# A decoder layer on Trainium2: finishing of the four widest top-k selections spread over the sparse-attention steps, the fourth settled by itself

## The reference

```python
rel = jax.nn.relu(jnp.einsum('bthd,bsd->bths', iqb, ik).astype(jnp.float32))
score = jnp.einsum('bths,bth->bts', rel, iwb.astype(jnp.float32)) * idx_scale
score = jnp.where(causal[None], score, -jnp.inf)
_, sel = lax.top_k(score, n_sel)
...
logits = jnp.where(valid[:, :, None, :], logits, -jnp.inf)
p = jax.nn.softmax(logits, axis=-1).astype(v.dtype)
```

## Time and profile before

| what | value |
|---|---|
| median of 3 runs | 1570.82 us (1570.29 to 1573.15) |
| the profiled execution | 1571.99 us |
| its span, first to last instruction | 1570.2 us |
| mean granted TensorE clock | 0.975 |
| TensorE, VectorE, ScalarE, GpSimd busy | 94%, 70%, 32%, 48% of the span |

### The profile page before, as it was taken

The page is one execution under the profiler, slowest core; times in us unless marked ns, Lnnn a source line. Parts: engine busy times, 40 slices in busy tenths (PEclk is TensorE's granted clock), DMA queues, the critical chain, the costliest instruction groups (busy, mean ns, idle before and its releaser), DMA issues.

```text
span 1570.2 us, 21084 instructions
## 1 busy us (share of the span) xinstructions
PE 1476.6 (94%) x7552; PEld 1255.9 (80%) x7552; DVE 1097.7 (70%) x2104; ACT 498.5 (32%) x1052; POOL 756.0 (48%) x583
## 2 busy tenths in 40 slices
PE   7999888889979999999999989999999999999997
PEld 6877667788868988777887778888888888888885
DVE  7578979788895432594434957777777777786857
ACT  3024567889536651122210211111111111111111
POOL 4240348566620003340333336777777777777622
PEclk9999999999979999999999999999999999999999
DMA  6445255555411004311111001111020202020202
GB/s 233 149 147 161 81 175 171 165 166 172 155 47 28 1 23 159 101 41 54 54 55 54 27 28 54 54 47 62 27 81 27 81 28 81 5 98 6 81 27 81
DMA packets 61479, 128.98 MB, mean 82 GB/s; under 512 B 6976, under 2 KB 34112, under 8 KB 53696
## 3 DMA queue, kind: packets, MB, share of 16 engines
q1 hardware_dynamic: 44352, 100.37, 19.4%
q10 hardware_dynamic: 17024, 27.27, 4.9%
HBM read 100.35 MB, written 27.26 MB: 81 GB/s over the span
## 4 chain that ended last, share of the span: by engine, by line
PE 73%; DVE 15%; issue 4%; ACT 4%; DMA 1%; POOL 1%; ACTq 0%; SPq 0%; DVEq 0%; POOLq 0%
PE banks L859 21%; PE banks L861 21%; PE banks L860 21%; PE banks L1059 3%; PE banks L913 2%; PE banks L914 2%; PE banks L1046 2%; DVE h_buf L2095 1%; ACT unread_late L1286 1%; PE banks L1068 1%; DVE bn L2081 1%; DVE act_lo L2074 1%; DVE score L1740 1%; DVE unread L1773 1%; PE banks L1015 1%
## 5 line engine op out<-in xcount | busy, mean ns | idle before, releaser
L769 POOL TENSOR_SCALAR w_hi<-raw 128x512 fp32r<-128x512 f32 x156 | 103.8, 693 | 459.6 <-PE banks L861 290.4
L2220 DVE TENSOR_TENSOR h_buf<-h_buf,banks 128x512 f32<-128x512 f32 x320 | 202.5, 678 | 13.1 <-PE banks L861 9.7
L774 POOL TENSOR_TENSOR w_lo<-raw,w_hi 128x512 fp32r<-128x512 f32 x156 | 210.2, 1382 | 0.0
L859 PE MATMUL banks<-act_hi,w_hi 128*128 128x512 f32 x512 | 200.1, 391 | 1.6 <-DVE act_lo L2074 1.6
L860 PE MATMUL banks<-act_lo,w_hi 128*128 128x512 f32 x512 | 199.9, 390 | 0.0
L861 PE MATMUL banks<-act_hi,w_lo 128*128 128x512 f32 x512 | 199.8, 390 | 0.0
L859 PE MATMUL banks<-w_hi,act_hi 128*128 128x512 f32 x384 | 153.2, 399 | 0.0
L859 PE MATMUL banks<-seven_hi,hid_hi 128*128 128x512 f32 x392 | 152.6, 389 | 0.0
L860 PE MATMUL banks<-seven_lo,hid_hi 128*128 128x512 f32 x392 | 152.5, 389 | 0.0
L861 PE MATMUL banks<-seven_hi,hid_lo 128*128 128x512 f32 x392 | 152.5, 389 | 0.0
L861 PE MATMUL banks<-w_hi,act_lo 128*128 128x512 f32 x384 | 150.6, 392 | 0.0
(11 more groups left out here) (220 smaller groups left out, 3530.1 us busy)
## 6 DMA issues: line engine op xcount, KB each, us to landing
raw<-w_down_dram SPq DMA_DIRECT2D x16, 1024.0 KB, 4.8
raw_up<-w_up_dram SPq DMA_DIRECT2D x14, 1024.0 KB, 4.8
q_tile<-qk_dram SPq DMA_DIRECT2D x176, 64.0 KB, 2.7
qk_dram<-q_hi ACTq DMA_DIRECT2D x28, 256.0 KB, 2.1
qk_dram<-roped ACTq DMA_DIRECT2D x28, 256.0 KB, 2.4
x_raw<-x_t_dram SPq DMA_DIRECT2D x8, 512.0 KB, 8.2
raw<-wk_mem_dram SPq DMA_DIRECT2D x4, 1024.0 KB, 6.5
raw<-wv_mem_dram SPq DMA_DIRECT2D x4, 1024.0 KB, 5.4
```

The source lines that it names most:

```text
L769: pool.tensor_scalar(w_hi[s][:, col], source[:, col], 1.0, 1.0, ALU.mult, ALU.mult)\
L774: pool.tensor_tensor(w_lo[s][:, col], source[:, col], w_hi[s][:, col].bitcast(F32), ALU.subtract).then_inc(w_ready, 1)
L859: pe.matmul(dst, lh, rh, start=(first and n == 0), stop=False)
L2220: ins = dve.tensor_tensor(out, out, ring_m[g % 6][:], ALU.add if way > 0 else ALU.subtract)
```

## The change

The generator's declared costs for `finish` are changed (0.2 us and a slope for each instruction, in place of a slope alone). The band budget is 2.1 us in place of 1.8; the sparse budget is by tile, 0.7 to 1.3 us in place of 2.0; and in the main loop what a step overspends or leaves is carried to the next. Settling is a function over a range of columns with yields between its parts. Column 2 is settled and finished by itself, straight after the narrow ones and without waiting for the wide ones; columns 3 to 5 are settled together after `wide_set`. The last two hunks of the diff make the forced path and the call of `select_for` fit.

```diff
@@ -205,7 +205,8 @@
     return range(N_EARLY_COUNTS + lo, N_EARLY_COUNTS + hi)
 
 
-NARROW_EARLY, BUDGET_BAND, BUDGET_DSA = 0.9, 1.8, 2.0
+NARROW_EARLY, BUDGET_BAND = 0.9, 2.1
+BUDGET_DSA = {2: 0.7, 3: 0.9, 4: 1.15, 5: 1.3, 6: 1.3, 7: 1.3}
 FIRST_PRODUCT = 2
 
 
@@ -1840,50 +1841,61 @@
                     col = slice(c, c + 1)
                     limit, rank, tie = threshold[:, col], tie_rank[:, 0:width], is_tie[c >= WIDE][:, 0:width]
                     chain(dve.tensor_scalar(score[i][:], score[i][:], sign[:, col], None, ALU.mult))
-                    yield width / 1700.0, None
+                    yield 0.2 + width / 1400.0, None
 
                     cost = tally(c, ALU.is_gt, limit, None)
                     dve.wait_ge(dve_step, written[-1])
                     chain(dve.tensor_scalar(ties[:, col], count[:, col], -1.0, float(TOPK), ALU.mult, ALU.add))
                     yield cost + 0.3, None
                     chain(dve.tensor_scalar(tie, score[i][:], limit, None, ALU.is_equal))
-                    yield width / 1700.0, None
+                    yield 0.2 + width / 1400.0, None
                     chain(dve.tensor_tensor_scan(rank, tie, tie, 0.0, ALU.add, ALU.bypass))
-                    yield width / 900.0, None
+                    yield 0.2 + width / 488.0, None
 
                     chain(dve.scalar_tensor_tensor(out=tie, in0=rank, scalar=ties[:, col], in1=tie,
                                                    op0=ALU.is_gt, op1=ALU.mult))
-                    yield width / 900.0, None
+                    yield 0.2 + width / 937.0, None
                     chain(dve.scalar_tensor_tensor(out=score[i][:], in0=score[i][:], scalar=limit, in1=tie,
                                                    op0=ALU.is_lt, op1=ALU.max))
-                    yield width / 900.0, None
+                    yield 0.2 + width / 937.0, None
                     chain(dve.tensor_scalar(score[i][:], score[i][:], MASKED, None, ALU.mult))
-                    yield width / 1700.0, i
+                    yield 0.2 + width / 1400.0, i
 
                 yield from bisect(EARLY, range(TOP_BIT, LAST_EARLY_BIT - 1, -1))
                 take_over(EARLY)
                 yield from bisect(WIDE, range(LAST_EARLY_BIT - 1, -1, -1))
                 yield from finish_narrow((0, 1))
+
+                def settle(lo, hi):
+
+                    cols = slice(lo, hi)
+                    if lo < WIDE:
+                        dve.wait_ge(dve_step, set_at[EARLY])
+                        chain(dve.tensor_scalar(plain[:, cols], trial[:, cols], 0, None, ALU.bitwise_xor))
+                    else:
+                        dve.wait_ge(trial_ready, len(EARLY_TILES) + len(COUNTS))
+                        chain(dve.tensor_scalar(plain[:, cols], trial[:, cols], SIGN_BIT, None, ALU.bitwise_xor))
+                    found = plain[:, cols].bitcast(F32)
+                    chain(dve.scalar_tensor_tensor(out=level[:, cols], in0=found, scalar=1.25 * 2.0 ** -24,
+                                                   in1=found, op0=ALU.mult, op1=ALU.add))
+                    yield 0.8, None
+                    for c in range(lo, hi):
+                        yield tally(c, ALU.is_ge, level[:, c:c + 1], minus_rank[:, c:c + 1]), None
+                    dve.wait_ge(dve_step, written[-1])
+                    chain(dve.tensor_tensor(level[:, cols], level[:, cols], found, ALU.subtract))
+                    chain(dve.scalar_tensor_tensor(out=level[:, cols], in0=count[:, cols], scalar=0.0,
+                                                   in1=level[:, cols], op0=ALU.is_ge, op1=ALU.mult))
+                    yield 0.8, None
+                    chain(dve.tensor_tensor(level[:, cols], level[:, cols], found, ALU.add))
+                    chain(dve.tensor_tensor(threshold[:, cols], sign[:, cols], level[:, cols], ALU.mult))
+                    yield 0.8, None
+
+                yield from settle(EARLY, WIDE)
+                yield from finish(EARLY)
                 while not wide_set[0]:
-                    yield 1e9, None
-
-
-                dve.wait_ge(trial_ready, len(EARLY_TILES) + len(COUNTS))
-                dve.wait_ge(dve_step, set_at[EARLY])
-                then(dve.tensor_scalar(plain[:, WIDE:N_SEL], trial[:, WIDE:N_SEL], SIGN_BIT, None, ALU.bitwise_xor))
-                chain(dve.tensor_scalar(plain[:, EARLY:WIDE], trial[:, EARLY:WIDE], 0, None, ALU.bitwise_xor))
-                found = plain[:, wide].bitcast(F32)
-                chain(dve.scalar_tensor_tensor(out=level[:, wide], in0=found, scalar=1.25 * 2.0 ** -24,
-                                               in1=found, op0=ALU.mult, op1=ALU.add))
-                for c in range(EARLY, N_SEL):
-                    yield tally(c, ALU.is_ge, level[:, c:c + 1], minus_rank[:, c:c + 1]), None
-                dve.wait_ge(dve_step, written[-1])
-                chain(dve.tensor_tensor(level[:, wide], level[:, wide], found, ALU.subtract))
-                chain(dve.scalar_tensor_tensor(out=level[:, wide], in0=count[:, wide], scalar=0.0,
-                                               in1=level[:, wide], op0=ALU.is_ge, op1=ALU.mult))
-                chain(dve.tensor_tensor(level[:, wide], level[:, wide], found, ALU.add))
-                chain(dve.tensor_tensor(threshold[:, wide], sign[:, wide], level[:, wide], ALU.mult))
-                for c in range(EARLY, N_SEL):
+                    yield None, None
+                yield from settle(WIDE, N_SEL)
+                for c in range(WIDE, N_SEL):
                     yield from finish(c)
 
             pending = []
@@ -1915,11 +1927,17 @@
             selection = select_keys()
             selected = set(range(FIRST_TOPK_TILE))
 
-            def select_for(us):
-
-                while us > 0 and len(selected) < NT:
-                    cost, tile = next(selection, (1e9, None))
-                    us -= cost
+            credit = [0.0]
+
+            def select_for(us, carry=False):
+
+                credit[0] = us + (credit[0] if carry else 0.0)
+                while credit[0] > 0 and len(selected) < NT:
+                    cost, tile = next(selection)
+                    if cost is None:
+                        credit[0] = 0.0
+                        return
+                    credit[0] -= cost
                     if tile is not None:
                         selected.add(tile)
                     if pending:
@@ -1931,7 +1949,8 @@
 
             def select_until(i):
                 while i not in selected:
-                    tile = next(selection)[1]
+                    cost, tile = next(selection)
+                    assert cost is not None
                     if tile is not None:
                         selected.add(tile)
 
@@ -2064,7 +2083,7 @@
                     split_memory(use)
                 set_all(counts_at(n - 1))
                 if n >= 2:
-                    select_for(BUDGET_BAND if n < NS else BUDGET_DSA)
+                    select_for(BUDGET_BAND if n < NS else BUDGET_DSA[DSA[min(n - NS, ND - 1)][0]], True)
                     flush()
 
             def low_groups(n, t, count):
```

## The result

| | before | after |
|---|---|---|
| median (lowest to highest) | 1570.55 us (1569.86 to 1573.15) | 1547.49 us (1544.65 to 1552.14) |
| ratio to before | 1 | 0.9853 [0.9824, 0.9882] |
| the profiled execution; its span | 1571.99; 1570.2 | 1552.14; 1550.3 |
| mean granted TensorE clock | 0.975 | 0.983 |

The change makes the kernel 23.1 us faster by the medians, 19.9 us by the two profiled executions. The forecast was 29.2 us and 1541.6 us; the measured median lies in the range, 5.9 us above the number. The profiled execution of after is the slowest of its four, so I ran the same kernel once more (the first experiment) and read both. One of the later versions, the kernel before with GpSimd held, had one execution of 1678.19 us at a granted clock of 0.838 among twelve; its ratio leaves that one out, and the other eleven lie between 1562.88 and 1569.47 us.

The account below looks back on a forecast made before the run. VectorE's queue, full of selection work, was taken to starve TensorE around 436 to 480 us. Gains of 6.3 + 23.2 - 0.3 = 29.2 us gave 1541.6 us, range 1538 to 1553 us.

Parts of the forecast that it names:

- The bound and its cure: Around 436 to 480 us VectorE's queue is full while TensorE starves, and idle behind; spreading selection work gains 29.2 us.
- The order of issue: Added-up generator yields: column 2 settled in steps 37 and 38, finished 39 to 45; wide columns settled in 46 to 52.
- Term A: Step 36: 3.9 us wait on normalising plus 2.6 us half-clock loss shrinks to 0.2 us; gain 6.3 us.
- Term B: Steps 40 to 51: 19.45 us undisturbed where the stage took 43.84, with 1.2 us left; gain 23.2 us.
- The step that failed: Settling in two goes: 12 small operations instead of 7, each 0.15 to 0.55 us, 0.8 to 2.8 in idle time.
- The cover of tiles 3 to 6: Moved selection work fits VectorE's idle time before masks; 0.3 us taken for tile 3, nothing shows in later tiles.
- Rival 3: Tiles 3 to 6 lose their cover: about 27 us of selection appears as waits, slower, 1579 us with 10 of clock; chance 0.03.
- Rival 1: VectorE stays late at steps 36 and 40 beside GpSimd: gain 19.8 us, 1551 us; chance 0.17.
- Rival 2: Clock stays low in tile 2 and early tile 3 through short idles: gain 9.7 us, 1561 us; chance 0.04.
- Rival 4: Gain given back at the first output products, weights or GpSimd late: 1571 us; chance 0.02.
- Rival 5: Pacing fails in the code, a tile forced in one piece at first use: about 5 us burst, 1547 us; chance 0.01.

Follow-up runs that it names:

- the first experiment: The changed kernel measured once more with no edit: 1544.87 us (1543.58 to 1549.43), ratio 0.9846.

## Why the prediction was right, and by how much it was off

**The bound and its cure: right.** VectorE's queue was full where TensorE starved and idle behind. The old sparse budget brings back 14.6 us, the split without the pacing brings nothing, and the pacing without the split brings as much as the change.

**The order of issue: right.** Column 2 is settled and its first finishing operations are issued in steps 37 to 39, and the wide columns' work lies between the masks of tiles 3 and on, as the added yields said.

**Term A, step 36: place right, size off.** The wait left is 1.58 us, not 0.2. The sum had 0.2 for the threshold, 1.5 for the sign, 1.5 for the equal and 1.1 for the normalising. Measured in after, VectorE in order of time, step 35 and the normalising of step 36:

```profile
417.10 1.26 DVE L1833 TENSOR_TENSOR threshold<-sign,trial 128x1 f32<-128x1 f32 x1
418.40 1.47 DVE L1843 TENSOR_SCALAR score<-score,sign 128x512 f32<-128x512 f32 x1
...
420.88 0.49 DVE L1850 TENSOR_SCALAR is_tie<-score,threshold 128x512 uint8<-128x512 f32 x1
421.40 1.13 DVE L2037 TENSOR_TENSOR sums<-sums,sink_exp 128x8 f32<-128x8 f32 x1
422.56 0.20 DVE L2038 RECIPROCAL inv_sum<-sums 128x8 f32<-128x8 f32 x1
422.79 0.69 DVE L2042 TENSOR_TENSOR h_buf<-banks,inv_sum 128x512 f32<-128x512 f32 x1
```

And GpSimd beside it:

```profile
417.05 5.45 POOL L775 TENSOR_TENSOR w_lo<-raw,w_hi 128x512 fp32r<-128x512 f32 x4
```

The two small operations cost 2.39 us where the sum had about 0.4, the equal 1.0 less than I gave it. No half clock followed: 424 to 428 us runs at 1.00. So this term gave 3.9 - 1.6 + 2.6 = 4.9 of 6.3 us.

**Term B, steps 40 to 51: size off at its start.** The wait left at step 40 is 1.64 us; I had 1.2 for it, by the wrong items. The sign took 0.76 and the normalising began without delay of its own, but three small operations of column 2's settling, which I had at 0.15 to 0.55 each and hidden, took 3.6 us and moved all of it back. (There are seven small operations around the counts in before, as the sum of 12 instead of 7 has it, and not the eight of the section on the kernel before.) Behind the wait came what the sum left out: clock 0.87, 0.50 and 0.77 in three stretches of 4 us. Their busy time times the missing clock is 2.36 x 0.13 + 4 x 0.50 + 4 x 0.23 = 3.2 us (1.6 in the second execution). Step 43, by the masks' starts 446.65 to 448.89, took 2.24 us where the sum had 2.19: there the clock is back.

**The shortfall closes.** Steps 34 to 52 were to take 43.0 and took 48.22: 5.2 us. Of these, 1.4 are the wait at step 36, 0.4 the wait at step 40, 3.2 the clock: 5.0. In the second execution 3.8 against 1.4 + 0.4 + 1.6 = 3.4. The first profiled execution also came 1.7 late into the band steps and lost 3.1 in steps 0 to 34, and gained 0.75 in steps 52 to 87: 5.2 + 1.7 + 3.1 - 0.75 is the 9.3 by which it fell short of 29.2. By the medians the gain is 6.1 us short in the first measurement and 4.1 in the second (25.1 us).

**The step that failed is one size**: "One is 0.15 to 0.55 us". The 0.51 to 0.55 were read in before from 436.12 to 438.38 us, and I took them for the cost beside GpSimd. What GpSimd ran there was not its subtraction, which begins at 438.33, but the shorter instruction ahead of it (before, GpSimd in order of time):

```profile
436.00 2.37 POOL L769 TENSOR_SCALAR w_hi<-raw 128x512 fp32r<-128x512 f32 x4 [0.53 <-PE banks L861]
```

One of these takes 2.37/4 = 0.59 us, and the four small operations that begin at 436.12 follow each other every 0.55 to 0.58. So they too lasted as long as GpSimd's instruction; in after the same operations fell beside the subtractions, and cost 1.21. The other is one term left out: I priced half clock behind the waits that go away, and not behind the one that I left in.

That a TENSOR_TENSOR with both inputs in SBUF waits for GpSimd is no surprise to the Trainium skill. Its page "SBUF — State Buffer", section "Who interferes with whom", says that a VectorE instruction with two SBUF inputs contends with a GpSimd instruction that reads SBUF, and that the loser is blocked for the other's whole instruction. The trace agrees: 1.21 against 0.16 us, in GpSimd's rhythm of 1.26. Had I applied it to the small operations, each beside a subtraction would have stood at about 1.2 in the sum.

**The cover of tiles 3 to 6: sufficient.** TensorE has no wait between 452 and 560 us; idle before the masks of tiles 4 and 5 fell from 9.6 to 2.8 and from 11.3 to 2.2 us, and something was left. Rival 3 is out. The last mask came at 555.31, 19.9 us earlier (29 forecast); the first 384-wide mask at 438.02, 3.9 earlier (6 forecast).

**The rivals.** Rival 1, VectorE late at steps 36 and 40, had the place right, and half of its price came true in steps 34 to 52 (5.2 of 9.4 us). It named the mechanism only as GpSimd beside other instructions. The median of the first measurement, 1547.49 us, is nearer to its 1551 than to the 1541.6 of the forecast; the second, 1544.87, is nearer to the forecast. Rival 2 is out: the clock is 1.00 in the 105 us from 460 us, and low only behind one wait, not through short idles in turn. Rival 4 is out: the rest is 994.96 and 994.99 us. Rival 5 is out: no first mask of a tile made TensorE wait.

**Open.** The entry into the band steps varied from 248.85 to 253.89 us between executions of the same rotary code. I did not look into it, and it is as large as most differences between the variants.

## What to carry to other kernels

Where one in-order engine does background work between operations that others wait for, compare its busy share before and behind the stall: full in front and idle behind means that pacing by what each step has room for, with the overdraft carried, gives the stall back without any work being removed. Here that was shown for the whole of it and for the sparse budgets, not for the carry or the costs by themselves. Price small two-input VectorE operations by the length of the GpSimd instruction beside them, not by their own size, and keep a chain of them away from GpSimd's reads or behind the deadline. And ask of every wait that a forecast leaves in whether a half-clock stretch comes with it, then ask what was hidden beneath the wait that goes: here a store with two buffers, which cost 3.4 us of wait and 1.5 of clock once VectorE was on time.

## What the runs showed of the hardware

Operations on one to eight columns with two inputs took 1.13 to 1.26 us beside GpSimd's TENSOR_TENSOR of 1.26 us, 0.51 to 0.55 beside its TENSOR_SCALAR of 0.59, and 0.16 without either; one that was issued in the middle of a subtraction took 0.59 (after, 407.60 us). Beside the TENSOR_TENSOR the count with an accumulator took 0.75 us (512 wide) and the one-input 128x1 operation 0.15. The wide one-input operations went either way: the sign took 1.47 us there (512 wide; 0.49 in before with GpSimd idle), the equal 0.49 in after and 1.56 in before (384 wide).

After waits of 1.6 to 1.8 us on the normalising at step 40 the clock fell in all four profiled executions that had one: in after to 0.50 in a stretch of 4 us, a loss of 3.2 us in all; in after again to 0.62 and 1.6 us; with the old sparse budget and with the third buffer alone to 0.50. After the wait of the same 1.6 us at step 36 it fell in none of them. Why at one and not at the other is open. With 1.2 us (step 35 skipped) or 0.9 us (pacing alone, or GpSimd held) of wait left at step 40 it did not fall; after 2.8 and 3.4 us for the store it did.
